# Second layer's memory and forgetting attention in one session, part of memory's product and two loads moved at the start

## What is computed

```python
def hybrid_layer(x, c_act, w_ada, b_ada, w_in, rel_bias, ...):
    mod = c_act @ w_ada + b_ada
    shift_mix, scale_mix, gate_mix, shift_ffn, scale_ffn, gate_ffn = jnp.split(mod, 6, axis=-1)
    proj = modulate(rms_norm(x), shift_mix, scale_mix) @ w_in
    qa, ka, va, qb, kb, vb = jnp.split(proj, cuts, axis=-1)
    oa = chunked_rel_attention(qa, ka, va, rel_bias)          # 8 heads
    ob = stick_breaking_attention(qb, kb, vb)                 # 8 heads
    mixed = concatenate([rms_norm(oa) * g_a, rms_norm(ob) * g_b]) @ w_out
    x = x + gate_mix * mixed
    return x + gate_ffn * ffn(modulate(rms_norm(x), shift_ffn, scale_ffn))

def memory_attention(q_mem, mem, mem_norm, w_mem_kv):
    kv = rmsnorm(mem, mem_norm) @ w_mem_kv                    # 256 x (256 of k, 256 of v)
    ...                                                       # 4 heads, softmax over 256

# second layer of the second block (k_sh, v_sh, log_f_cum come from the layer before)
z = rmsnorm(x, b_norm1) @ b_w_q                               # 768 + 256 columns
tok = forgetting_attention(z[..., :768], k_sh, v_sh, log_f_cum)   # 12 heads, causal
mem_o = memory_attention(z[..., 768:], mem, b_mem_norm, b_w_mem_kv)
x = x + concatenate([tok, mem_o]) @ b_w_out
x = x + conv_ffn(rmsnorm(x, b_norm2), ...)
```

## Time and profile before

| | us |
|---|---|
| median of 3 runs | 1900.61 |
| lowest, highest | 1895.25, 1902.62 |
| the profiled execution | 1899.79 |
| its span, first to last instruction | 1898.1 |
| its mean granted PE clock | 0.975 |

### The profile page before, as it was taken

How to read it: one execution, slowest core, us unless ns; L and a number is a source line. 1 busy time by engine, 2 the same in 40 slices (tenths; PEclk the granted TensorE clock), 3 DMA queues, 4 the chain that set the end, 5 groups by cost and what they waited for, 6 DMA issues and landing times.

```text
span 1898.1 us, 23166 instructions
## 1 busy us (share of the span) xinstructions
PE 1825.3 (96%) x8662; PEld 1466.3 (77%) x8662; DVE 1086.7 (57%) x1559; ACT 714.7 (38%) x988; POOL 38.8 (2%) x76
## 2 busy tenths in 40 slices
PE   6999988999999999999999999999998999999996
PEld 5888644778888888877888888888776788888884
DVE  5475655565565425764767774244576467776334
ACT  4311565343434323443443443241354344344220
POOL 3010000000000000000000000000000000000000
PEclk8999789999999999999999999999998999999997
DMA  9586000423232233322322322233401232232321
GB/s 339 179 318 224 23 1 1 134 79 108 88 98 101 78 105 91 103 67 67 109 90 90 109 88 92 91 96 92 153 23 45 67 111 89 88 110 83 106 77 44
DMA packets 152681, 192.67 MB, mean 102 GB/s; under 512 B 3534, under 2 KB 144152, under 8 KB 149164
## 3 DMA queue, kind: packets, MB, share of 16 engines
q1 hardware_dynamic: 146184, 154.23, 25.0%
q0 software_dynamic: 6288, 37.56, 5.4%
q10 hardware_dynamic: 148, 0.05, 0.0%
HBM read 187.58 MB, written 4.24 MB: 101 GB/s over the span
## 4 chain that ended last, share of the span: by engine, by line
PE 89%; DVE 5%; ACT 3%; DMA 2%; issue 1%; POOL 0%; DVEq 0%; ACTq 0%
PE bank L716 22%; PE bank L718 22%; PE bank L717 22%; PE bank L779 2%; PE bank L781 2%; PE bank L780 2%; PE bank L902 2%; PE bank L879 2%; PE bank L862 2%; PE bank L759 1%; PE bank L760 1%; PE bank L761 1%; DMA w_mem<-in_a_w_mem_kv 1%; PE bank L739 1%; PE bank L738 1%
## 5 line engine op out<-in xcount | busy, mean ns | idle before, releaser
L1679 DVE TENSOR_TENSOR w_lo<-w_stage,w_hi 128x2048 fp32r<-128x2048 f32 (+3 forms) x139 | 305.8, 2200 | 474.4 <-ACT w_hi L1290 474.3
L716 PE MATMUL bank<-act_hi,w_hi 128*128 128x512 f32 x1248 | 488.0, 391 | 1.3 <-DVE act_lo L1725 0.7
L718 PE MATMUL bank<-act_hi,w_lo 128*128 128x512 f32 x1248 | 485.7, 389 | 0.0
L717 PE MATMUL bank<-act_lo,w_hi 128*128 128x512 f32 x1248 | 485.6, 389 | 0.0
L1290 ACT ACTIVATE w_hi<-w_stage 128x2048 fp32r<-128x2048 f32 (+2 forms) x141 | 259.2, 1839 | 513.2 <-PE bank L718 436.6
L716 PEld LDWEIGHTS bank<-act_hi,w_hi 128*128 128x128 f32 x1248 | 234.3, 188 | 53.2 <-DVE act_lo L1725 2.3
L718 PEld LDWEIGHTS bank<-act_hi,w_lo 128*128 128x128 f32 x1248 | 234.3, 188 | 49.1
L717 PEld LDWEIGHTS bank<-act_lo,w_hi 128*128 128x128 f32 x1248 | 234.3, 188 | 48.4 <-issue 0.5
L716 PE MATMUL bank<-mid_hi,w_hi 128*128 128x512 f32 x528 | 205.4, 389 | 0.0
L718 PE MATMUL bank<-mid_hi,w_lo 128*128 128x512 f32 x528 | 205.4, 389 | 0.0
L717 PE MATMUL bank<-mid_lo,w_hi 128*128 128x512 f32 x528 | 205.4, 389 | 0.0
(11 more groups left out here) (367 smaller groups left out, 2418.1 us busy)
## 6 DMA issues: line engine op xcount, KB each, us to landing
ada_stage<-in_w_ada POOLq DMA_DIRECT2D x24, 1024.0 KB, 7.4
w_stage<-in_w_up SPq DMA_DIRECT2D x22, 1024.0 KB, 5.1
w_stage<-in_a_ffn_in SPq DMA_DIRECT2D x22, 1024.0 KB, 5.0
w_stage<-in_b_ffn_in SPq DMA_DIRECT2D x22, 1024.0 KB, 5.0
w_stage<-in_w_in SPq DMA_DIRECT2D x12, 1024.0 KB, 5.7
w_stage<-in_w_down SPq DMA_DIRECT2D x8, 1024.0 KB, 5.1
w_stage<-in_a_ffn_out SPq DMA_DIRECT2D x8, 1024.0 KB, 5.2
w_stage<-in_b_ffn_out SPq DMA_DIRECT2D x8, 1024.0 KB, 5.0
```

The lines of the kernel that those rows point to most:

```text
L716: pe.matmul(dst, wh, mh, start=start and k == 0, stop=False)
L717: pe.matmul(dst, wh, ml, start=False, stop=False)
L718: last = pe.matmul(dst, wl, mh, start=False, stop=stop and k == nk - 1)
L1679: dve.tensor_tensor(w_lo[slot][:, 0:n], w_stage[slot][:, 0:n], w_hi[slot][:, 0:n].bitcast(FP32), ALU.subtract).then_inc(w_ready, 1)
```

## The change

**Last layer.** `fox` and `mem_b` become one session `b` of 32 units: the 8 memory units first, then the 24 forgetting units, at the same lags. So the chunk with the memory queries is loaded and multiplied first. Of the 24 Q quarters two stand beside each memory unit and one beside each of the first eight forgetting units; beside the other 16 there is nothing. In the last four steps, which have no new scores, stands the product of the first output tile of b_out with the tiles of the contraction that are ready, [6,7], [0,1], [2,3], [4]; then tile 5, the second output tile, and the whole second chunk. This tile's bank is another, so the update of x swaps two banks. The output staging takes the place of two other buffers, and the splits of the weights are put at other steps.

**Start.** The v-product of memory leaves the start. Its weights are loaded behind w_out's second chunk, and its activations, now parked in DRAM too, come back from there. Its first half stands between the last values of `rel` and the first stick-breaking tail sum, its second half between the tail sum of unit 1 and the scores of unit 3, and DVE's copies of it beside unit 3. The first four tiles of raw x are turned ahead of the column sum, which goes to another bank. On POOL, slices 6 and 7 of w_ada are issued ahead of the small loads, and both parks ahead of slice 8; SP starts to load w_in when the slice with index 5 has come, before with index 4. DVE's first qkv copy waits for both parks.

The diff, cut to what acts on the order (the rest renames sessions and passes bank numbers on):

```diff
-SESSIONS = [("rel", 4, True), ("mem_a", 2, False), ("fox", 6, True), ("mem_b", 2, False)]
+SESSIONS = [("rel", 4, True), ("mem_a", 2, False), ("b", 8, True)]
...
-            sp.wait_ge(ada_loaded[4], 16)
+            sp.wait_ge(ada_loaded[5], 16)
...
+            w_out = rows("w_out")
+            for j in range(4):
+                if j == 2:
+                    sp.wait_ge(w_ready, C0["w_out"] + 2)
+                    load_mem(1)
+                    sp.wait_ge(mem_parked, 32)
+                    sp.dma_start(mem_again[0][:, :, :].rearrange("p k n -> p (k n)"), park_dram.ap()[0])\
+                        .then_inc(mem_unparked[0], 16)
+                    sp.wait_ge(mem_done, 2)
+                load(C0["w_out"] + j, cols(w_out, 0, KT, CHUNK_COLS * j), KT, CHUNK_COLS, j % 2)
...
-            stream("b_q", rows("b_w_q_2"), 2)
+            for j, n0 in enumerate((TOK, 0, CHUNK_COLS, 2 * CHUNK_COLS)):
+                load(C0["b_q"] + j, cols(rows("b_w_q_2"), 0, KT, n0), KT, CHUNK_COLS, j % 2)
...
-            small_loads()
             ada(6, first[6])
             ada(7, first[7])
+            small_loads()
...
             pool.wait_ge(w_loaded[1], 16)
+            pool.wait_ge(tr_saved, TR0["mem"] + KT)
+            for l in range(2):
+                pool.dma_start(park_dram.ap()[l], mem_scaled[:, l, :, :].rearrange("p k n -> p (k n)"))\
+                    .then_inc(mem_parked, 16)
...
                 if k == 1:
-                    pool.wait_ge(tr_saved, TR0["mem"] + KT)
-                    pool.dma_start(park_dram.ap(), mem_scaled[:, 1, :, :].rearrange("p k n -> p (k n)"))\
-                        .then_inc(mem_parked, 16)
-                    pool.wait_ge(mem_saved, 2)
-                    mem_store(0)
+                    pool.wait_ge(mem_saved, 1)
+                    mem_store(0, [0])
...
+            pool.wait_ge(mem_saved, 2)
+            mem_store(0, [1])
+            pool.wait_ge(mem_stored, 32)
             pool.wait_ge(act_ready, SPLIT0["w_out"] + 8)
-            pool.wait_ge(mem_parked, 16)
-            pool.dma_start(mem_again[:, :, :].rearrange("p k n -> p (k n)"), park_dram.ap())\
-                .then_inc(mem_unparked, 16)
+            pool.wait_ge(mem_parked, 32)
+            pool.dma_start(mem_again[1][:, :, :].rearrange("p k n -> p (k n)"), park_dram.ap()[1])\
+                .then_inc(mem_unparked[1], 16)
...
+                if qi == 0 and pair > PAIR0["b"]:
+                    pe.wait_ge(out_saved, pair)
+                elif qi == 0 and pair == PAIR0["b"]:
+                    pe.wait_ge(group_free, G0["b_q"] + 1)
...
-                    if x and name == "fox" and x["qi"] == 0 and t:
-                        pair = t // 4
-                        if pair == 1:
-                            pe.wait_ge(group_free, G0["b_q"] + 1)
-                        else:
-                            pe.wait_ge(q_saved, pair)
+                    if x and name == "b" and x["qi"] == 0 and t >= 8:
+                        pe.wait_ge(q_saved, t // 4 - 1)
...
             mem_half(0, 0)
             mem_half(0, 1)
-            pe.wait_ge(w_mem_loaded[1], 16)
-            mem_half(1, 0)
             pe.wait_ge(xn_saved, KT)
+            turn_x(range(4))
             pe.wait_ge(consts_set, 14)
             pe.wait_ge(ada_added, 8)
-            ada_sum(range(16), bank[5])
-            mem_half(1, 1)
+            ada_sum(range(16), bank[3])
...
             for j in range(4):
                 chunk(C0["qk_a"] + j, j % 2, KT, CHUNK_COLS, act, g=G0["qk_a"] + j, gslot=j % 2,
                       tile_wait=normed("w_in") if j == 0 else None,
-                      chunk_wait=(mem_saved, 2) if j == 1 else None)
+                      chunk_wait=(mod_ready, 1) if j == 1 else None)
                 if j == 0:
-                    pe.wait_ge(mod_ready, 1)
+                    pe.wait_ge(x_saved, 4)
                     pe.wait_ge(conv_loaded, 16 * 4 * len(CONVS))
                     for b in range(2):
                         batch("conv", b, [(vec_rows[0:sizes[i], i, :], P * (i - 2 - 3 * b))
                                           for i in range(2 + 3 * b, 5 + 3 * b)])
-                if j in (1, 2):
+                if j == 1:
                     pe.wait_ge(tr_saved, TR0["conv"] + 2)
-                    turn_x(range(4 * j - 4, 4 * j))
+                    turn_x(range(4, 8))
...
             softmax("rel", meanwhile=[first_sb])
+            pe.wait_ge(w_mem_loaded[1], 16)
+            pe.wait_ge(mem_unparked[0], 16)
+            pe.wait_ge(out_saved, 3)
+            mem_half(1, 0)
             for u in range(SB_UNITS):
                 sb_tail_sum(u)
+                if u == 1:
+                    pe.wait_ge(out_saved, 4)
+                    mem_half(1, 1)
+                if u == 4:
+                    pe.wait_ge(mem_saved, 2)
...
+            def q_quarter(n):
+
+                tile, quarter = n // 4, n % 4
+                c = C0["b_q"] + 1 + tile // 2
                 if quarter == 0:
                     pe.wait_ge(w_ready, c + 1)
-                    if tile == 2:
-                        pe.wait_ge(group_free, G0["b_q"] + 1)
-                    else:
-                        pe.wait_ge(q_saved, tile - 1)
+                    pe.wait_ge(q_saved, tile)
                 part(c, c % 2, tile % 2, range(2 * quarter, 2 * quarter + 2), q_act, start=quarter == 0,
                      stop=quarter == 3, dst=bank[1][:, :], first_done=q_tile)
 
-            pe.wait_ge(group_free, G0["b_q"])
+            B_OUT_KS = [[6, 7], [0, 1], [2, 3], [4]]
+
+            def b_beside(t):
+
+                for n in (2 * t, 2 * t + 1) if t < 8 else (8 + t,) if t < 16 else ():
+                    q_quarter(n)
+                if t == 32:
+                    pe.wait_ge(w_ready, C0["b_out"] + 1)
+                    pe.wait_ge(q_saved, 6)
+                if t >= 32:
+                    part(C0["b_out"], 0, 0, B_OUT_KS[t - 32], o_b, tile_wait=o_b_low, start=t == 32,
+                         dst=bank[1][:, :])
+
+            pe.wait_ge(group_free, G0["b_q"] + 1)
             pe.wait_ge(f_saved, 1)
-            pe.wait_ge(q_saved, 1)
-            softmax("fox", beside=q_quarter)
             pe.wait_ge(mem_back, 64)
-            pe.wait_ge(q_saved, 7)
-            def o_b(k):
-                return o_hi_b[:, k, :], o_lo_tok[:, k, :] if k < 6 else o_lo_mem[:, k - 6, :]
-
-            def early_b(m):
-                pe.wait_ge(out_low, 2 + PAIR0["mem_b"] - PAIR0["fox"])
-                early("b_out", m, o_b)
-
-            softmax("mem_b", meanwhile=[lambda: early_b(0), lambda: early_b(1)])
-            late("b_out", o_b)
+            softmax("b", beside=b_beside)
+            part(C0["b_out"], 0, 0, [5], o_b, tile_wait=o_b_low, stop=True, dst=bank[1][:, :])
+            part(C0["b_out"], 0, 1, range(8), o_b, start=True, stop=True, dst=bank[0][:, :])
+            pe.wait_ge(scores_read, 2 * N_UNITS)
+            pe.wait_ge(w_ready, C0["b_out"] + 2)
+            for m in range(2):
+                part(C0["b_out"] + 1, 1, m, range(8), o_b, start=True, stop=True)
+            gemm_pairs("b_out", 2, o_b, None, first=1)
...
+            save_x(range(4))
...
-            mem_group(1)
...
                 c = C0[ph] + j
-                if ph == "qk_a" and j == 2:
-                    dve.wait_ge(mem_parked, 16)
+                if ph == "qk_a" and j == 0:
+                    dve.wait_ge(mem_parked, 32)
...
+                if u == 3:
+                    mem_group(1)
...
+            norm_group(C0["b_q"], first_tiles(G0["b_q"]), 0, lambda m: q_b[:, 6 + m, :], rms, HD ** -0.5)
...
+            def b_beside(t):
+                if t == 8:
+                    dve.wait_ge(decay_back, 16)
+                if t in (2, 4, 6, 8, 12, 16):
+                    q_evict(t // 2 - 1 if t < 12 else t // 4 + 1)
+                if t < 4:
+                    split_quarter(C0["b_q"] + 2, t)
+                if t in (6, 7):
+                    split_quarter(C0["b_q"] + 3, 2 * (t - 6))
+                    split_quarter(C0["b_q"] + 3, 2 * (t - 6) + 1)
+                for c, t0 in ((C0["b_out"], 11), (C0["b_out"] + 1, 19)):
                     if t0 <= t < t0 + 4:
                         split_quarter(c, t - t0)
...
-            softmax("fox", beside=fox_beside)
             dve.wait_ge(zero_set, 2)
-            softmax("mem_b", beside=mem_beside)
+            dve.wait_ge(decay_stored, 16)
+            softmax("b", beside=b_beside)
```

159 lines of the change are left out of this document (66 added, 93 removed).

## The result

| | before | after |
|---|---|---|
| median, us | 1900.82 (4 runs) | 1887.10 (4 runs) |
| lowest, highest | 1895.25, 1902.62 | 1886.09, 1891.54 |
| the profiled execution | 1899.79 | 1887.10 |
| its span | 1898.1 | 1885.4 |

The ratio is 0.9943, with a 95% interval of 0.9916 to 0.9971: the changed kernel is 0.6% faster. Forecast were 1889.3 us and a range of 1882.5 to 1896.5.

The account below looks back on a forecast made before the run. PE bounds the kernel (busy 1825.3 of 1898.1 us), so only its idle time and half clock can shrink. 6.1 + 1.8 - 2.8 + 6.2 = 11.3 off 1899.79, plus 0.8 to the median, gives 1889.3 us; range 1882.5 to 1896.5.

Parts of the forecast that it names:

- Column sum: Start: the adaptive-norm sum starts 6.6 us earlier, at 39.8, less 0.5 for half clock: 6.1 us saved (4.3 to 7.2).
- my best case: Start: the 2.87 us wait for w_ada goes and DVE runs through, ending the last slice at 38.7.
- Turns: Start: the first four turns of x move from between two dense chunks into PE's pause: 1.8 us saved.
- Parks: Start: two parks in DRAM land by 68 to 70 ahead of DVE's first qkv copy; cost nothing, cover 3 us.
- The rival: Start: parks of 11 us each land at 80 and PE loses 8; gain 3.3, 1897 us, chance 0.05.
- Stick-breaking: The moved v-product lands here: 0.3 plus 3.5 us lost, 1.0 back as clock; net 2.8 lost (1.5 to 5.5).
- the forecast's sign: Stick-breaking: DVE takes unit 3's scores 2.5 to 3.5 us after it has ended unit 2's.
- Attention: Second layer: pauses and half clock worth 15.9 us removed, 9.7 added; net 6.2 us saved (2 to 11).
- First wait: Second layer's attention: the session starts when both Q tiles of the first chunk are copied out; 0.9 us added.
- Low parts: Attention tail: waits for low parts of contraction tiles k=4 and k=5, 0.6 and 2.1 us added.
- Slower: Second layer's attention: clock falls in the 16 unfilled units and stays down; four pairs cost 32 us, 1921, chance 0.05.
- Less: Moved product at half clock and unfilled units 10.6 us a pair: gain 4.6 us, 1896, chance 0.25.

Follow-up runs that it names:

- again: The changed kernel unaltered, run once more beside the kernel before: 1887.78 us, ratio 0.9949.
- loads_as_before: The changed kernel with the ten small loads ahead of w_ada's slices 6 and 7 on POOL again: 1889.52 us, ratio 0.9961.
- attention_alone: The kernel before with only the last layer's part of the change: 1891.23 us, ratio 0.9962.

## Why the prediction was right, point by point

**Total.** Forecast 11.3 us less in the profiled execution, measured 12.7; 11.5 less at the median's level (1889.3 against 1900.82), measured 13.7 (10.5 in `again`, beside other runs of the kernel before). Direction, mechanism and sum hold, and the median lies below the 1891 that the forecast called faster (0.55). That the sum came so close is in part luck: over the profiles the start gave less than forecast (6.7 of 7.9 us), the last layer mostly more, and the stretch between them varies by 6.3 us with the place where the clock falls.

**Column sum.** I let it start 6.6 earlier, at 39.8; it started at 38.7, my best case, 7.7 earlier, because the slices came in time (`loads_as_before` shows that most of it is POOL's order). I added 0.5 for half clock; it was 2.5, since all 32 passes run at it. This is the worst-sized term. Its two errors nearly cancel: 5.3 measured for 6.1. Over the profiles it is 4.9, from 66.8 us (before and `attention_alone`) to 61.9 (seven with the new start and order, without the extra transposes). The earlier trace rows had the measure: 16 passes behind a pause took 6.49 us there where 32 took 7.07 at full clock; I took the 4.34 of a sum that had work ahead of it.

**Turns.** 1.8 forecast; 123.8 - 122.0 = 1.8 measured, in every profile.

**Parks.** DVE's first qkv copy waited 2.2 us for them and started at 69.14, within the 68 to 70 forecast; PE's next work, the turns, began at 73.80 without a pause, and DVE's conv copies before it had ended at 71.4: the cover was 2.4 us where I had 3. The rival is out.

**Stick-breaking.** First half: 0.3 late forecast, 0.2 measured (3.49 us from the end of `rel` to the first tail sum, before 3.32). Second half: 2.5 (3.5 less 1.0 of clock) forecast, 3.45 less 0.7 or 1.6 measured. DVE waited 2.79 us for unit 3's scores, as the forecast's sign had it. Net -2.8 forecast, 0.0 in the first profile, -2.6 between a mean over eight profiles and one over two. The step that I had left out is chance: behind stick-breaking's pauses the clock falls in some executions and not in others, and a fall costs 1.7 to 2.9 us (unit 3's tail sums to the next scores take 4.90 us in after and 3.20 before, unit 7's 6.11 before and 3.20 after), so no single profile can show a net of 2.8.

**Attention.** 6.2 forecast, 6.6 measured in five profiles, 5.1 in two. First wait 0.9: 0.8. A memory unit 4.6: 4.6. Waits for Q tiles 1.4: 1.4. Four pairs without quarters 3 x 9.6 + 11.1 = 39.9: 8.83 + 12.57 + 9.59 + 9.59 = 40.6. Low parts 0.6 and 2.1: 0.6 and 2.1. The third output chunk waits for nothing. Of the slow pair I had named the load (DVE's four quarters); a wait of DVE in its own order, behind ACT's half, started it, and half clock made up the rest. The total was right within 0.7 us, of the slow pair 1.5 were missing (11.1 forecast), and its cause was only half named.

**The rivals.** "Slower", the clock down throughout the pairs without quarters, did not come: it was 1.00 in three and 0.86 in one. "Less" needed 10.6 a pair; three were below 9.6. The 0.76 of the stretch at 252 to 256 was 1.00 in the first profile after, and this isn't chance: in all twelve profiles with the first half ahead of unit 0 the clock stayed at 1.00 from the end of `rel` to unit 3's scores, and in both without it it fell at unit 0. The forecast's reason for the 1.0 us holds.

## What to carry to other kernels

Price work by where it lands, pause by pause: a half product of 3.5 us cost nothing ahead of unit 0, its full length behind unit 1, 1.0 ahead of unit 7, and work put one step beside a pause cost its full length. Read the length of short pieces behind a pause at half clock, and look for work, useful or not, that can stand in the pause. When a wait is removed, the clock may still fall behind the next long pause (1.6 of 1.9 us in one profile here), so fill that one too: with both gone no fall was left in this stage in four profiles. The useless work ahead of the column sum only put the fall off; it can pay where a short piece of the critical path then gets through at full clock. And compare stages over several profiles before a net of a few us is believed.

## What the runs showed of the hardware that I had not expected

The granted clock's falls are not a function of the program. In 14 profiles the pauses ahead of the tail sums of units 3, 7, 11, 14 and 15 were as long each time (1.5 to 1.9, 2.6, 1.5, 1.7, and 0.5 or 2.1 us, where nothing had been moved into them), yet unit 3's sum was slow in 7, unit 7's in 6, unit 15's in 5, unit 11's in none, and unit 14's in 6. Two executions of one program differed by 3.2 us from the first score of `rel` to the third memory product. When unit 14 had the fall, unit 15's pause was 0.5 instead of 2.1 us, so that a fall there cost nearly nothing. The three kernels with no product, or only an eighth of it, behind unit 1's tail sum but with the first half ahead of unit 0 had no fall at units 3, 7 and 15 (one had it at 14). Whether that is cause or chance stays open: three profiles are few, and fillers in those pauses weren't tried. At unit 0 it is clearer: in or behind the pause of 3.32 us the clock fell in both profiles that have it, and in none of the twelve in which the first half fills it. In the attention stage, with its pauses of at most 0.8 us but for two, every unit repeated to 0.1 us; only behind the last of these pauses (2.08 us) did the clock fall in some profiles and not in others. And in all 14 the clock fell inside a column sum of 64 one-column passes that followed dense work without a pause.
